# Order of the low halves, the merge's adds, the idle products, the first expert's rows and the gather's scaling in a two-layer decoder trunk

## What is computed

```python
for l in range(2):
    h = rmsnorm(x, norm_mix[l])
    qa, ka, va, qb, kb, vb, qi, ki, wi, qc, kc, vc, g = _split(h @ w_in[l], IN_SIZES)
    o_a = stick_breaking_attention(qa, ka, va)               # 4 heads
    o_b = dsa_attention(...)     # an indexer picks 64 keys per query, then softmax
    o_c = sliding_window_attention(...)  # window 128, 8 heads, with sinks
    gates = sigmoid(g + b_gate[l])                           # 3 x 1024 per token
    merged = (gates[0] * (o_a @ w_pa[l]) + gates[1] * (o_b @ w_pb[l])
              + gates[2] * (o_c @ w_pc[l]))
    x = x + merged @ w_out[l]
    x = x + cross_attention(rmsnorm(x), rmsnorm(mem), ...)   # 4 heads, 256 memory tokens
    hf = rmsnorm(x, norm_ffn[l])
    x = x + (swiglu(hf) if l == 0 else moe_swiglu(hf))       # dense; then the top 2 of 8 experts
```

## Time and profile before

| | |
|---|---|
| median of 3 runs | 1763.64 us (1762.31 to 1764.25) |
| the profiled execution | 1761.99 us |
| its span, first to last instruction | 1760.4 us |
| TensorE busy | 1702.5 us, 97% |
| VectorE busy | 1391.7 us, 79% |
| ScalarE busy | 1104.0 us, 63% |
| GpSimd (POOL) busy | 92.9 us, 5% |
| mean granted TensorE clock | 0.991 |

### The profile page before, as it was taken

How to read it: one execution, slowest core, us unless ns; L and a number is a source line. 1 busy time by engine, 2 the same in 40 slices (tenths; PEclk the granted TensorE clock), 3 DMA queues, 4 the chain that set the end, 5 groups by cost and what they waited for, 6 DMA issues and landing times.

```text
span 1760.4 us, 22594 instructions
## 1 busy us (share of the span) xinstructions
PE 1702.5 (97%) x7816; PEld 1366.5 (78%) x7816; DVE 1391.7 (79%) x1367; ACT 1104.0 (63%) x1076; POOL 92.9 (5%) x73
## 2 busy tenths in 40 slices
PE   7999898999999999899999999999999999999999
PEld 5777777888777787777888888888888888888876
DVE  5799767545477987668898888888888888888897
ACT  4646355443355453557777777777777777777765
POOL 1100110000001001010000000000000000000440
PEclk9999999999999999999999999999999999999999
DMA  8533494554455335349999999999999999999985
GB/s 301 215 104 130 176 364 149 212 191 169 150 182 182 120 138 204 134 173 399 366 381 366 366 381 369 366 383 365 364 385 363 381 363 368 380 367 366 409 340 195
DMA packets 74113, 498.14 MB, mean 283 GB/s; under 512 B 8256, under 2 KB 9024, under 8 KB 17872
## 3 DMA queue, kind: packets, MB, share of 16 engines
q1 hardware_dynamic: 66560, 467.60, 69.4%
q0 software_dynamic: 7360, 29.87, 4.6%
q10 hardware_dynamic: 144, 0.03, 0.0%
HBM read 481.73 MB, written 15.73 MB: 283 GB/s over the span
## 4 chain that ended last, share of the span: by engine, by line
PE 83%; DVE 8%; ACT 3%; issue 2%; DVEq 2%; DMA 2%; POOL 0%; ACTq 0%; POOLq 0%; SPq 0%
PE ps L588 26%; PE ps L582 26%; PE ps L578 25%; DVE w_lo L416 3%; PE ps L804 1%; ACT w_hi L411 1%; DVE w_lo L1022 1%; PE ps L508 1%; PE ps L1348 1%; DMA rows_of_experts<-scratch,row_no 1%; DVE st L1673 0%; DMA z<-rows_of_experts 0%; DVEq L1676 0%; PE ps L1271 0%; DMA raw<-in_layer_tiles 0%
## 5 line engine op out<-in xcount | busy, mean ns | idle before, releaser
L1022 DVE TENSOR_TENSOR w_lo<-raw,w_hi 128x2048 fp32r<-128x2048 f32 x168 | 391.6, 2332 | 65.9 <-ACT w_hi L939 65.8
L578 PE MATMUL ps<-w_hi,hT_hi 128*128 128x512 f32 (+1 forms) x1520 | 427.1, 403 | 10.4 <-ACT hT_hi L550 4.6
L1022 DVE TENSOR_TENSOR w_lo<-z,w_hi 128x2048 fp32r<-128x2048 f32 x168 | 386.8, 2304 | 45.8 <-ACT w_hi L939 44.7
L588 PE MATMUL ps<-w_lo,hT_hi 128*128 128x512 f32 (+1 forms) x1520 | 413.2, 394 | 7.2 <-DVE w_lo L416 7.1
L582 PE MATMUL ps<-w_hi,hT_lo 128*128 128x512 f32 (+1 forms) x1520 | 413.0, 394 | 1.0 <-DVE hT_lo L557 0.9
L939 ACT ACTIVATE w_hi<-z 128x2048 fp32r<-128x2048 f32 x168 | 321.7, 1915 | 43.2 <-PE ps L588 38.3
L588 PEld LDWEIGHTS ps<-w_lo,hT_hi 128*128 128x128 f32 x1520 | 283.5, 189 | 77.3 <-DVE w_lo L416 9.9
L582 PEld LDWEIGHTS ps<-w_hi,hT_lo 128*128 128x128 f32 x1520 | 284.1, 189 | 70.2 <-DVE hT_lo L557 2.1
L939 ACT ACTIVATE w_hi<-raw 128x2048 fp32r<-128x2048 f32 x168 | 321.0, 1911 | 25.5 <-PE ps L588 25.5
L578 PEld LDWEIGHTS ps<-w_hi,hT_hi 128*128 128x128 f32 x1520 | 272.5, 189 | 67.8 <-ACT hT_hi L550 5.5
L416 DVE TENSOR_TENSOR w_lo<-raw,w_hi 128x2048 fp32r<-128x2048 f32 (+2 forms) x111 | 248.3, 2242 | 77.0 <-ACT w_hi L411 75.2
(11 more groups left out here) (295 smaller groups left out, 993.8 us busy)
## 6 DMA issues: line engine op xcount, KB each, us to landing
...
```

Of the source, the lines that this page charges most:

```text
L578: pe.matmul(acc, hi[:, k, cols], wh, start=start and j == 0, stop=False)
L588: ins = pe.matmul(acc, hi[:, k, cols], wl, start=False, stop=stop and j == len(hk) - 1)
L1022: v.tensor_tensor(w_lo[:, ring, :], moe_raw(p), w_hi[:, ring, :].bitcast(F32), ALU.subtract) \
```

## The change

The edits, in the order of the program: in layer 0 the gains of half 0 stand ahead of the first slot's halves on ScalarE and VectorE; one w_lo moves from behind the row maxima to ahead of them; VectorE adds the second mixer's product itself, and the w_lo of the merge stand at other places; a copy in the cross-attention moves ahead of a w_lo; in layer 1's first block the eviction stands ahead of a w_lo (`take_first`); the idle products are three in other places and not four; the first expert's rows are turned after chunk (1, 1) and not before it; POOL scales by TENSOR_TENSOR with the gate broadcast instead of TENSOR_SCALAR.

```diff
--- before.py
+++ after.py
@@ -345,7 +345,7 @@
                 pool.wait_ge(sem(f"y_back{k}"), 16)
                 if j:
                     pool.wait_ge(sem("x_part"), i + 1)
-                pool.tensor_scalar(yg[:, k, :], yg[:, k, :], g_other[:, j, i:i + 1], None, ALU.mult)
+                pool.tensor_tensor(yg[:, k, :], yg[:, k, :], bc(g_other[:, j, i:i + 1], [P, D]), ALU.mult)
                 pool.drain()
                 pool.tensor_tensor(x_sb[:, i, :], x_sb[:, i, :], yg[:, k, :], ALU.add).then_inc(sem("x_part"), 1)

@@ -363,16 +363,6 @@
             pool.tensor_tensor(bias[:, 0, 4:6, :], bias[:, 0, 4:6, :], bc(window.unsqueeze(1), [P, 2, 2 * P]), ALU.add)
             pool.tensor_tensor(bias[:, 1, :, :], bias[:, 1, :, :], bc(window.unsqueeze(1), [P, 6, 2 * P]), ALU.add)
             pool.drain().then_inc(sem("bias_ready"), 1)
-
-        def pb_prod(b, i):
-            return sc[:, 2048 + (2 * b + i) * NB:2048 + (2 * b + i + 1) * NB]
-
-        def pool_merge(pool, l):
-            for b in range(2):
-                for i in range(TT):
-                    m = xn[:, i, b * NB:(b + 1) * NB]
-                    pool.wait_ge(sem("pb_prod"), 4 * l + 2 * b + i + 1)
-                    pool.tensor_tensor(m, m, pb_prod(b, i), ALU.add).then_inc(sem("pb_added"), 1)

         def pool_program(pool):
             load_head_gains(pool, 0)
@@ -393,7 +383,6 @@
                 load_bias(pool, l)
                 add_window(pool, l)
                 load_cross_gains(pool, l)
-                pool_merge(pool, l)
             pool.wait_ge(sem("merged"), L)
             pool.dma_start(gain_row, t["norm_ffn"][L - 1:L].to_broadcast([P, D])).then_inc(sem("gain_row"), 16)
             pool_moe(pool)
@@ -618,12 +607,13 @@
                 pe_block_slot(pe, s + n, k0 + 4 * h, h == 0, h == per - 1 or plan[s + n][1] == KC, blk0[name, l] + b, x_lo,
                               hi, lo, between[1] if between and between[0] == n else None)

-        def dve_linear(v, cnt, name, l, take, limit, b0=0, b1=None):
+        def dve_linear(v, cnt, name, l, take, limit, b0=0, b1=None, take_first=False):

             s, nblk, per = slots_of(name, l)
             for b in range(b0, b1 or nblk):
                 last = s + (b + 1) * per - 1
-                ahead(dve_split_to, v, cnt, last - 1, limit)
+                if not take_first:
+                    ahead(dve_split_to, v, cnt, last - 1, limit)
                 blk = blk0[name, l] + b
                 v.wait_ge(sem("tile0_done"), blk + 1)
                 take(b, 0).then_inc(sem("evac"), 1)
@@ -859,8 +849,11 @@
                 pe_moe_chunk(pe, ip, par, 0, 0, ("hg_L", n + 1))
             pe_moe_chunk(pe, ip, par, 0, 1)
             pe_moe_chunk(pe, ip, par, 1, 0)
-            pe_turn_rows(pe, n + 1)
+            if not first_expert(ip, par):
+                pe_turn_rows(pe, n + 1)
             pe_moe_chunk(pe, ip, par, 1, 1)
+            if first_expert(ip, par):
+                pe_turn_rows(pe, n + 1)
             with pe.Fori(2, N_MOE // 2) as u:
                 pe_moe_chunk(pe, ip, par, u, 0)
                 pe_moe_chunk(pe, ip, par, u, 1)
@@ -928,7 +921,9 @@
                 chunk(0, 0)
             chunk(0, 1, None if first else "y")
             chunk(1, 0)
-            chunk(1, 1, "rows")
+            chunk(1, 1, None if first else "rows")
+            if first:
+                hook("rows")
             with fori(2, N_MOE // 2) as u:
                 chunk(u, 0)
                 chunk(u, 1)
@@ -1385,10 +1380,10 @@
                     if i == 1 and b == 0:
                         pe_turn_tile(pe, l, 0)

-        def pe_idle_products(pe, n):
+        def pe_idle_products(pe, n, bank=7):

             for _ in range(n):
-                pe.matmul(ps[:, 7, :], ident, x_sb[:, 0, 0:NB], start=True, stop=True)
+                pe.matmul(ps[:, bank, :], ident, x_sb[:, 0, 0:NB], start=True, stop=True)

         def pe_program(pe):

@@ -1445,9 +1440,11 @@
                     pe_turn_half(pe, "mix", x_sb, 0)
                 if l == 0:
                     pe_dense(pe, FFN0[0], N_DENSE, turn_next)
+            pe_idle_products(pe, 1, 0)
             pe_turn_tile(pe, L - 1, 1)
+            pe_idle_products(pe, 1, 0)
             pe_logits(pe, 1)
-            pe_idle_products(pe, 2)
+            pe_idle_products(pe, 1)
             pe.wait_ge(sem("chosen"), 1)
             pe.matmul(ps[:, 6, 0:8], before_tri, chosen[:, 0, :], start=True, stop=True)
             pe.matmul(ps[:, 6, 8:16], ones, chosen[:, 0, :], start=True, stop=False)
@@ -1598,8 +1595,8 @@
                     act.wait_ge(sem("ident_in"), 16)
                     act.activation(warm, ident[:, 0:1], ACT.Copy)
                     act.wait_ge(sem("gains"), 16)
+                    act_hi_gain(act, "mix", l, hT_hi, part=(0,))
                     act_split_to(act, cnt, s0 + 1)
-                    act_hi_gain(act, "mix", l, hT_hi, part=(0,))
                     act.wait_ge(sem("x1_in"), 16)
                     act_squares(act, x_sb, 0, "mix_squares")
                     act_hi_gain(act, "mix", l, hT_hi, part=(1,))
@@ -1766,6 +1763,7 @@
             dve_split_to(v, cnt, g0 + 3)
             dve_gate(v, l, 0, 0)
             dve_masked(v, l, 0, 1, between=0)
+            dve_split_to(v, cnt, g0 + 4)
             dve_row_max(v, l, 1)
             dve_split_to(v, cnt, g0 + 5)
             dve_topk_rounds(v, 0, 1)
@@ -1850,7 +1848,9 @@
                     last = s + (b + 1) * per - 1
                     blk = blk0[name, l] + b
                     for i in range(TT):
-                        if not (j == 1 and b == 0 and i == 1 or j == 2 and b == 1 and i == 1):
+                        if j == 1 and b == 1 and i == 1:
+                            dve_split_to(v, cnt, min(last + RING - 1, lim))
+                        elif not (j == 1 or j == 2 and b == 1 and i == 1) or b == i == 0:
                             dve_split_to(v, cnt, min(last + RING - 1 + i, lim))
                         if i == 0:
                             v.wait_ge(sem("tile0_done"), blk + 1)
@@ -1858,14 +1858,10 @@
                             v.wait_ge(sem("mm_done"), last + 1)
                         g = gates[:, i, j * D + b * NB:j * D + (b + 1) * NB]
                         m = xn[:, i, b * NB:(b + 1) * NB]
-                        prod = pb_prod(b, i) if j == 1 else sc[:, 4096 + i * NB:4096 + (i + 1) * NB]
+                        prod = sc[:, 2048 + i * NB:2048 + (i + 1) * NB]
                         v.tensor_tensor(prod if j else m, ps[:, LIN + i, :], g, ALU.mult).then_inc(sem("evac"), 1)
-                        if j == 1:
-                            v.drain().then_inc(sem("pb_prod"), 1)
-                        else:
-                            v.drain()
-                        if j == 2:
-                            v.wait_ge(sem("pb_added"), 4 * l + 2 * b + i + 1)
+                        v.drain()
+                        if j:
                             ins = v.tensor_tensor(m, m, prod, ALU.add)
                     if j == 2:
                         ins.then_inc(sem(("merged_half", "merged")[b]), 1)
@@ -1933,9 +1929,9 @@
             v.drain()
             dve_cross_probs(v, l, 0)
             dve_cross_max(v, l, 1)
-            dve_split_to(v, cnt, s + 3)
             v.wait_ge(sem("x_probs_T"), 2 * l + 1)
             v.tensor_copy(xPT[:, 1, :, 0:P], psXT[0][:, 1, :, :]).then_inc(sem("x_pT_dve"), 1)
+            dve_split_to(v, cnt, s + 3)
             dve_cross_probs(v, l, 1)
             v.wait_ge(sem("x_probs_T"), 2 * l + 2)
             v.tensor_copy(xPT[:, 1, :, P:S], psXT[1][:, 1, :, :]).then_inc(sem("x_pT_dve"), 1)
@@ -2063,10 +2059,9 @@
                 s0 = blocks["in", l]
                 if l == 0:
                     v.wait_ge(sem("gains"), 16)
+                dve_lo_gain(v, "mix", l, hT_hi, hT_lo, part=(0,))
                 if l == 0:
                     dve_split_to(v, cnt, s0 + 1)
-                dve_lo_gain(v, "mix", l, hT_hi, hT_lo, part=(0,))
-                if l == 0:
                     v.wait_ge(sem("mix_squares"), 2)
                     dve_rsqrt(v, "mix", D, norm_rs[:, 0:2])
                     dve_lo_gain(v, "mix", l, hT_hi, hT_lo, part=(1,))
@@ -2081,7 +2076,7 @@
                 v.drain()
                 if l == L - 1:
                     v.wait_ge(sem("rows_put"), 16)
-                dve_linear(v, cnt, "in", l, take_in(v), gate0[l], b1=1)
+                dve_linear(v, cnt, "in", l, take_in(v), gate0[l], b1=1, take_first=l > 0)
                 if l == 0:
                     v.wait_ge(sem("mem0_in"), 16)
                     v.wait_ge(sem("mem_squares"), 2)
```

## The result

The changed kernel takes 1768.19 us (14 runs, 1766.36 to 1769.69), the kernel before 1764.72 in the runs beside it (14 runs, 1761.79 to 1767.38): ratio 1.0022, 95% interval 1.0014 to 1.0029, that is 3.9 us slower (2.5 to 5.1). The forecast was 4.1 slower, 1767.7.

What follows compares the result with a forecast made beforehand. TensorE, busy for 97% of the span, was taken as the bound, so edits counted by its waits. The terms summed to +4.1 us on the profiled 1761.99: 1766.1, or 1767.7 as a median, with an overall range of 1761.0 to 1771.5.

Steps and rivals of the forecast that it cites:

- A: Start of layer 0: the reordered gains and halves let TensorE reach its third product earlier, -1.0 us.
- B: Masked scores, both layers: w_lo comes sooner, but the eviction is waited for and the turning's time holds, +0.2 us.
- E: Entry of layer 1: the wait for tile 0's eviction goes, w_lo comes as much later, -0.1 us.
- C: Merge, both layers: w_lo freed of POOL's adds shortens TensorE's waits, -3.5 us.
- D: Cross-attention: the copy moves ahead of w_lo, but TensorE waits for ScalarE's scratch, 0 us.
- F: Idle products around the router: faster logits, then TensorE idles before the ranks and its last products slow, +0.8 us.
- G: First expert's rows: the DMA wait goes, but ScalarE's copy delays the next chunk's w_hi, +3.0 us.
- H: Gather at the end on POOL: scalings by TENSOR_TENSOR slow VectorE's w_lo like additions, reaching TensorE, +4.7 us.
- Worse: Rival for the last gather and first expert's rows: POOL's gap goes and slow clock follows, together +7.4 us; chance 0.15.
- The swap as free for VectorE: Rival for the last gather: POOL's operation costs VectorE by bytes, not kind; sum -0.6 us, 1763.0; chance 0.15.
- G as free: Rival for the first expert's rows: ScalarE gets them without waiting, -1.4 instead of +3.0 us, sum -0.3; chance 0.10.
- The other side, faster: Rival for the last gather: shorter POOL scalings no longer hold additions back into later w_lo, -4.4 us, 1759.2; chance 0.10.

Runs made afterwards that it cites:

- merge_alone: The kernel before with only the merge's edit (VectorE adds, POOL's adds gone, low halves one eviction later): 1764.71 us, ratio 1.0004.
- idle_back: The changed kernel with two idle products behind the logits again and none ahead of the turning and the logits: 1767.1 us, ratio 1.0020.
- scalar_back: The changed kernel with POOL scaling by TENSOR_SCALAR again: 1763.11 us, ratio 0.9994.
- scaling_alone: The kernel before with only POOL's scaling changed to TENSOR_TENSOR: 1767.59 us, ratio 1.0023.
- rows_alone: The kernel before with only the first expert's rows turned after chunk (1, 1): 1767.13 us, ratio 1.0018.
- rows_back: The changed kernel with the first expert's rows turned before chunk (1, 1) again: 1762.65 us, ratio 0.9994.
- halves_merge: The changed kernel with the rows' turning, POOL's scaling and idle products undone; the halves' order and VectorE's merge adds stay: 1761.75 us, ratio 0.9992.
- idle_4: halves_merge with one idle product ahead of the turning, one ahead of the logits, four behind them: 1765.28 us, ratio 1.0010.
- rows_mid: halves_merge with TensorE turning the first expert's rows inside chunk (1, 1), ScalarE and VectorE copying behind it: 1759.22 us, ratio 0.9969.

## Why the prediction was right

The table has the stages, in us, over all 14 profiles: the range with the edit out and with the edit in (the last three rows are for one edit each).

```
stage                                        edit out         edit in       change   forecast
A  turning to third product, layer 0         10.46 - 11.41     8.90 -  9.11   -2.0      -1.0
B  third product to turning, layer 0        130.22 - 131.34  130.13 - 131.04  -0.3      +0.2
B, E  layer 1 to its first eviction         176.54 - 176.59  176.50 - 177.64  +0.3      -0.1
C  merge, both layers                        50.30 -  50.65   46.62 -  46.65  -3.9      -3.5
D  merge to cross-attention, layer 0         57.46 -  58.03   57.48 -  58.70  +0.8        0
F  last rows' turning to prefix matmuls      18.46 -  20.26   20.26 -  20.28  +1.3      +0.8
G  prefix matmuls to last expert's rows     880.48 - 887.79  884.44 - 884.87  +3.5      +3.0
H  last expert's rows to last wait           97.51 -  99.28  101.80 - 102.69  +3.4      +4.7
```

(For G the change is against the 881.2 of both profiles of before; the gap of the means over eight and four profiles is 2.0. In D merge_alone counts as out. F leaves out the runs with four idle products behind the logits, H the one without scalings. The other changes are of means. The forecast for B is for both layers, in its first row.) With -0.4 in layer 1's cross-attention (68.3 to 67.9 from the merge to the turning of the last rows) they add up to +2.7; measured were +3.9 (2.5 to 5.1), forecast +4.1. So the forecast had the right terms at work, but that its sum is within 0.2 of the measured one is luck: by the stages A, B and C gained 1.9 more than forecast, H cost 1.3 less, and D, E, F and G cost 2.2 more; the layer 1 cross-attention, in no term, gave 0.4.

Point by point. **A** was right in its mechanism and too small: the third product's stretch is 9.1, 1.35 below the 10.46 I worked from where 1.0 was forecast, and the other four profiles with the old order need 10.9 to 11.4, so the trace I worked from was the best of five. **B** was right: the wait of 3.4 moved to the eviction. **C** was right to 0.4, each wait within 0.35, and it is what merge_alone repeats. **D** was wrong: I set it at nothing, because TensorE waits for ScalarE there. It does, but in eight of nine profiles with the new order the eight turnings behind that wait run at the slow clock for longer (1.59 to 1.92, the changed kernel's 1.91 at 0.50; in the five with the old order 1.04 to 1.31, before's 1.04 at 1.00). Whether the order does it or the earlier arrival from the merge isn't separated: merge_alone, earlier but in the old order, has 57.48, and so has idle_back, the one of the nine with the new order. **E** was right: the wait went to tile 1 (1.44 at 499.28 in the changed kernel). **F** was right in its mechanism (2.91 idle, ranks and products slow) and somewhat small in the trace (1.8 for 0.8; the section on the change counts three idle products for four, but the two behind the ranks stay, so that there are five for four); in the median idle_back and the changed kernel can't be told apart. **G** was right in its step: a wait of 2.91 for w_hi (forecast 3.1), then 0.19 and 0.40 (0.4 and 0.8). What I took as fixed was the other side, the 1.38 it removes; that is a draw of 0 to 6.3, and with the other edits of this change it is mostly another number. **H** was right in kind (each scaling now stops VectorE as an addition does) and too large: 3.4 for 4.7. What VectorE loses did reach TensorE in full; the price of a scaling was too high. Over 2.29 each, VectorE's w_lo lose 12.3 us to POOL in the changed kernel and 9.2 before, 3.1 more where 4.6 was forecast. The w_lo beside the four scalings take 2.88, 3.64, 3.64 and 3.98, not the 3.8 to 4.5 of those beside additions, since the new scaling runs for 1.90 and an addition for 2.39.

The rivals. *Worse* is out: POOL's gap stays (9.52 us), and H and G are 3.4 and 3.5 instead of 7 and 4. The swap as free for VectorE is out by scalar_back and scaling_alone. G as free is out by rows_alone.

The other side, faster, is out too: a w_lo loses up to 0.6 to a scaling by TENSOR_SCALAR, and in the changed kernel's profile 0.6 to 1.7 to one by TENSOR_TENSOR. But the prediction took the recorded 4.88 for the scaling's own time. The scaling began at 1673.68 while a w_lo ran that ended at 1675.85, and ended 2.72 after that; alone the first one took 2.88. So 2.2 of the 4.88 were waiting for VectorE, and the additions were held back by that wait.

For w_lo and POOL's TENSOR_TENSOR the traces show that the one that begins second waits for the other's end. In the 14 profiles 88 w_lo began while such an operation ran on POOL, and all 88 ended 2.15 or 2.16 after it; an addition of 128x1024 that began beside a running w_lo ended 2.23 to 2.36 after it, a scaling by TENSOR_TENSOR 1.75 or 1.76. For TENSOR_SCALAR they show it in one direction alone. It waits for w_lo as the others do, but a w_lo that begins while it runs, with 1.8 to 2.5 us of it left, loses 0 to 0.6. Why isn't shown. VectorE's split of the turned activations (L1026, one of its inputs in PSUM) took 0.42 at 1649.30 with POOL at no such work, and 0.41 at 1680.51 beside POOL's scaling.

Not additive: rows_back (-4.9), scalar_back (-4.9) and both with the idle products (-5.3). The profiles give G and H 3.5 and 3.4, and H stays so without G's edit (101.80 and 102.13) and with it (102.28 and 102.69). What varies from profile to profile is the wait at the old place: 0 in the profiles of rows_back and halves_merge, 6.3 in idle_4, 4.7 in merge_alone. halves_merge's runs lie in two heaps (1759.1 to 1761.8 and 1764.0 to 1765.5), and merge_alone's in two as well, as wide apart as such a wait. That each upper run had that wait is inferred, since one run of each kernel was profiled: a lower one of halves_merge, without a wait, and an upper one of merge_alone, with 4.68. rows_mid takes the wait away, and its six runs lie in one heap (1756.9 to 1760.0).
